# Layer 1's retention: decayed queries made by VectorE from the turned queries, scores over 128 rows of zero-padded keys, the retention's steps sooner

## The reference, cut to what matters

```
n = arange(128);  diff = n[:, None] - n[None, :]
dmat  = where(diff >= 0, exp(log_g * diff), 0)      # within a chunk
xi    = exp(log_g * (n + 1))                        # decay of a query's row
zeta  = exp(log_g * (127 - n))                      # decay of a key's row
inner = ((qc @ kc.T) * dmat) @ vc
cross = (qc * xi[:, None]) @ state
state = exp(log_g * 128) * state + (kc * zeta[:, None]).T @ vc
out   = rms(forward + backward);  mixed = out * silu(gate)
```

## Time and profile before

| what | value |
|---|---|
| median of 3 runs | 814.98 us (814.67 to 816.67) |
| span of the profiled execution | 811.6 us |
| median less span | 3.4 us |
| TensorE busy | 805.4 us, 99% |
| VectorE busy | 634.0 us, 78% |
| ScalarE busy | 339.9 us, 42% |
| GpSimd busy | 187.8 us, 23% |

### The profile page before, as it was taken

One profiled execution on the slowest core, in us unless ns is written; L12 is line 12 of the kernel. 1 busy time (PEld: TensorE's weight loads), 2 busy tenths in 40 slices (PEclk: granted clock), 3 DMA queues, 4 the chain that ended last, 5 costly groups with the idle time before them and its releaser, 6 DMA issues.

```text
span 811.6 us, 11794 instructions
## 1 busy us (share of the span) xinstructions
PE 805.4 (99%) x4364; PEld 691.4 (85%) x4364; DVE 634.0 (78%) x1112; ACT 339.9 (42%) x721; POOL 187.8 (23%) x189
## 2 busy tenths in 40 slices
PE   9999999999999999999999999999999999999998
PEld 7788888888888888888888888888889988999986
DVE  5998778768984476885578788978798678599998
ACT  4374465632122254342545544551134222455580
POOL 2222111111121221122324555544260114000000
PEclk9999999999999999999999999999999999999999
DMA  7236644445143322336868677596935634866562
GB/s 241 88 96 233 233 155 156 151 161 182 53 156 114 95 78 78 90 93 130 177 144 163 140 151 161 131 182 135 202 104 183 182 98 135 235 184 183 184 203 78
DMA packets 132862, 120.47 MB, mean 148 GB/s; under 512 B 4749, under 2 KB 100550, under 8 KB 132806
## 3 DMA queue, kind: packets, MB, share of 16 engines
q1 hardware_dynamic: 124326, 102.94, 40.9%
q0 software_dynamic: 8448, 16.78, 12.4%
q10 hardware_dynamic: 32, 0.01, 0.0%
HBM read 117.62 MB, written 35.65 MB: 189 GB/s over the span
## 4 chain that ended last, share of the span: by engine, by line
PE 92%; DVE 5%; issue 1%; ACT 1%; DMA 1%; POOL 0%; DVEq 0%; ACTq 0%
PE proj L1886 23%; PE proj L1888 23%; PE proj L1887 23%; PE bank_t L1900 3%; PE bank_o L1975 2%; DVE x L1592 1%; PE score L1888 1%; PE score L1887 1%; PE score L1886 1%; DVE w_lo L1247 1%; PE score L2050 1%; PE score L1960 1%; PE score L1961 1%; PE score L2049 1%; PE bank_o L2068 1%
## 5 line engine op out<-in xcount | busy, mean ns | idle before, releaser
L1247 DVE TENSOR_TENSOR w_lo<-w_raw,w_hi 128x1024 fp32r<-128x1024 f32 x151 | 192.0, 1274 | 44.3 <-POOL w_hi L778 36.1
L778 POOL TENSOR_SCALAR w_hi<-w_raw 128x1024 fp32r<-128x1024 f32 x101 | 118.6, 1174 | 438.6 <-DMA w_raw<-in_w_in_dram 314.6
L1886 PE MATMUL proj<-xt_hi,w_hi 128*128 128x512 f32 (+1 forms) x448 | 171.2, 382 | 0.0
L1888 PE MATMUL proj<-xt_hi,w_lo 128*128 128x512 f32 (+1 forms) x448 | 168.1, 375 | 0.0
L1887 PE MATMUL proj<-xt_lo,w_hi 128*128 128x512 f32 (+1 forms) x448 | 167.8, 374 | 0.0
L1888 PEld LDWEIGHTS proj<-xt_hi,w_lo 128*128 128x128 f32 x448 | 84.4, 188 | 15.6
L1887 PEld LDWEIGHTS proj<-xt_lo,w_hi 128*128 128x128 f32 x448 | 84.5, 189 | 14.1
L1886 PEld LDWEIGHTS proj<-xt_hi,w_hi 128*128 128x128 f32 x448 | 84.5, 189 | 14.0
L1886 PE MATMUL proj<-w_hi,xt_hi 128*128 128x512 f32 x152 | 60.9, 401 | 0.2 <-ACT prob L1012 0.2
L1888 PE MATMUL proj<-w_hi,xt_lo 128*128 128x512 f32 x152 | 59.5, 391 | 0.0
L1887 PE MATMUL proj<-w_lo,xt_hi 128*128 128x512 f32 x152 | 59.4, 391 | 0.0
(11 more groups left out here) (471 smaller groups left out, 1871.2 us busy)
## 6 DMA issues: line engine op xcount, KB each, us to landing
w_raw<-in_w_in_dram SPq DMA_DIRECT2D x79, 512.0 KB, 3.8
w_sums<-in_w_in_dram SPq DMA_DIRECT2D x8, 1024.0 KB, 7.0
w_sums<-w_sums POOLq DMA_DIRECT2D x8, 1024.0 KB, 9.1
w_raw<-w_sums SPq DMA_DIRECT2D x16, 512.0 KB, 3.8
w_raw<-w_sums SPq DMA_DIRECT2D x32, 256.0 KB, 3.3
w_raw<-in_w_out_dram SPq DMA_DIRECT2D x14, 512.0 KB, 3.3
w_raw<-in_w_in_dram SPq DMA_DIRECT2D x26, 256.0 KB, 3.3
w_sums<-in_w_attn_out_dram SPq DMA_DIRECT2D x4, 1024.0 KB, 6.5
```

What stands on the lines that cost most here:

```text
L778: pool.tensor_scalar(hi, raw, 1.0, 1.0, ALU.mult, ALU.mult).then_inc(hi_done, 1)
L1247: dve.tensor_tensor(lo, raw, hi.bitcast(F32), ALU.subtract).then_inc(w_split, 1)
L1886: pe.matmul(out, left[0], right[0], start=first, stop=False)
L1888: return pe.matmul(out, left[1], right[0], start=False, stop=last)
```

## The change

- RN 2 and 3 go, and with them `q_decay` and the four turns RT 2 to 5 of decayed queries. RT is now 0 and 1 (keys, g = 17), 2 and 3 (plain queries, g = 18).
- VectorE makes the decayed queries from the turned plain ones: for RT 2 and 3, four products each of 64 partitions by 512, PSUM bank times `decays`, a table along the tokens repeated for the four chunks. They count in `q_decayed`. In VectorE's list they stand behind AN 3.
- `decays` (2 directions, 4 heads, 128 tokens) is prepared at g = 2 and, two products for each head, at g = 4 to 10, and ScalarE takes its exponential at g = 12. `ret_c` and `steps_to` shrink accordingly; four one-column memsets for `half_of` are added at g = 2.
- ScalarE copies each bank of turned keys twice into `rk_own`, once for each of its two heads, with a scale by partition that is 1 in the head's half and 0 in the other. RS then takes all 128 rows of keys and queries.
- KV 0 waits for all four RT copies, for both `q_decayed` and for the decayed keys.
- `RET_FIRST` goes from 22 to 20, so KV, RS, RA and RB are two step times sooner; F 6 and F 7 move from g = 34 and 36 to 32 and 34, the other F stay.

```diff
-RET_FIRST = DA_STEPS + 6
+RET_FIRST = DA_STEPS + 4
...
-    if g == DA_STEPS:
-        out += [("RN", 2), ("RN", 3)]
     x = 2 * (g - DA_STEPS - 1)
-    if 0 <= x < 8:
+    if 0 <= x < 4:
         out += [("RT", x), ("RT", x + 1)]
...
-    finals = {21: 0, 22: 1, 23: 2, 25: 3, 27: 4, 29: 5, 34: 6, 36: 7}
+    finals = {21: 0, 22: 1, 23: 2, 25: 3, 27: 4, 29: 5, 32: 6, 34: 7}
...
                 act.wait_ge(rt_done, m + 1)
-                if m == 6:
+                if m == 0:
+                    act.wait_ge(halves_set, 4)
+                if m == 2:
                     act.wait_ge(av_done, DA_STEPS)
-                dst = rkT[:, m, :] if m < 2 else q_decT[:, m - 2, :] if m < 6 else rqT[:, m - 6, :]
-                act.activation(dst, score[:, m % 2, :], ACT.Copy).then_inc(rt_free, 1)
+                if m < 2:
+                    for c in range(2):
+                        last = act.activation(rk_own[:, 2 * m + c, :], score[:, m % 2, :], ACT.Copy, scale=half_of[:, c:c + 1])
+                else:
+                    last = act.activation(rqT[:, m - 2, :], score[:, m % 2, :], ACT.Copy)
+                last.then_inc(rt_free, 1)
...
+                        act.activation(decays[:], decays[:], ACT.Exp).then_inc(decay_done, 1)
...
+                for c in range(2):
+                    here, there = halves(c)
+                    dve.memset(half_of[here, c:c + 1], 1.0).then_inc(halves_set, 1)
+                    dve.memset(half_of[there, c:c + 1], 0.0).then_inc(halves_set, 1)
...
+                done(dve.tensor_scalar(decays[:, 0, last_row, :], diff[:, CENTRE:CENTRE + P], minus_p, 1.0, ALU.subtract, ALU.add))
+                done(dve.tensor_scalar(decays[:, 1, last_row, :], decays[:, 0, last_row, :], -1.0, P + 1.0, ALU.mult, ALU.add))
...
+                for c in range(2):
+                    dve.tensor_scalar(decays[:, c, h, :], decays[:, c, RET_HEADS - 1, :], log_g[:, 4 * c + h:4 * c + h + 1], None, ALU.mult)
...
+                    elif kind == "RT" and m >= 2:
+                        if m == 2:
+                            dve.wait_ge(decay_done, 3)
+                        dve.wait_ge(rt_done, m + 1)
+                        for c in range(2):
+                            here, h = slice(c * HD, (c + 1) * HD), 2 * (m - 2) + c
+                            for d in range(2):
+                                last = dve.tensor_tensor(q_decT[d * HD:(d + 1) * HD, h, :].rearrange("p (s q) -> p s q", s=ST),
+                                                         score[here, m % 2, :].rearrange("p (s q) -> p s q", s=ST),
+                                                         decays[here, d, h, :].unsqueeze(1).broadcast_to([HD, ST, P]), ALU.mult)
+                        last.then_inc(q_decayed, 1)
...
                     if m == 0:
-                        pe.wait_ge(rt_free, 8)
+                        pe.wait_ge(rt_free, 4)
+                        pe.wait_ge(q_decayed, 2)
+                        pe.wait_ge(ret_scaled, 2)
...
-                    r = slice((m % 2) * HD, (m % 2 + 1) * HD)
                     for c in range(ST):
-                        last = pe.matmul(score[:, 1, c * P:(c + 1) * P], rkT[r, m // 2, c * P:(c + 1) * P],
-                                         rqT[r, m // 2, c * P:(c + 1) * P], start=True, stop=True)
+                        last = pe.matmul(score[:, 1, c * P:(c + 1) * P], rk_own[:, m, c * P:(c + 1) * P],
+                                         rqT[:, m // 2, c * P:(c + 1) * P], start=True, stop=True)
```

More of the change, by code:

```diff
@@ L346, in build @@
         scoring.close()
-        q_decay = sb("q_decay", [P, ST, RET_HEADS, 2, HD], stack=one)
+        rk_own = sb("rk_own", [P, RET_HEADS, S], stack=one)
         q_decT = sb("q_decT", [P, RET_HEADS, S], stack=one)
@@ L369, in build @@
         diff = sb("diff", [P, TAB], stack=one)
-        rkT = sb("rkT", [P, 2, S], stack=one)
         k_decay = sb("k_decay", [P, ST, RET_HEADS, 2, HD], stack=one)
         dmat = sb("dmat", [P, RET_HEADS, P], stack=one)
+        decays = sb("decays", [P, 2, RET_HEADS, P], stack=one)
         lam_s = sb("lam_s", [P, 2], stack=one); lam_e = sb("lam_e", [P, 2], stack=one); neg_lam = sb("neg_lam", [P, 1], stack=one)
@@ L377, in build @@
         dec_z = sb("dec_z", [P, 8], stack=one); dec_q = sb("dec_q", [P, 8], stack=one); dec_p = sb("dec_p", [P, 8], stack=one)
-        log_g = sb("log_g", [P, 8], stack=one); steps_to = sb("steps_to", [P, 4], stack=one)
-        ret_c = sb("ret_c", [P, 6, RET_HEADS], stack=one); rs_k = sb("rs_k", [P, ST], stack=one)
+        log_g = sb("log_g", [P, 8], stack=one); steps_to = sb("steps_to", [P, 2], stack=one); half_of = sb("half_of", [P, 2], stack=one)
+        ret_c = sb("ret_c", [P, 4, RET_HEADS], stack=one); rs_k = sb("rs_k", [P, ST], stack=one)
         neg_log_b = sb("neg_log_b", [P, 4], stack=one)
@@ L603, in build @@
         decay_arg = sem("decay_arg"); decay_done = sem("decay_done")
-        ret_scaled = sem("ret_scaled")
+        ret_scaled = sem("ret_scaled"); q_decayed = sem("q_decayed"); halves_set = sem("halves_set")
         rt_done = sem("rt_done"); rt_free = sem("rt_free")
@@ L1306, in prepare_decays @@
                 minus_p = diff[:, CENTRE:CENTRE + 1]
-                for k, (sign, steps) in enumerate(((-1.0, 1.0), (1.0, P), (1.0, P - 1.0), (-1.0, 0.0))):
+                for c in range(2):
+                    here, there = halves(c)
+                    dve.memset(half_of[here, c:c + 1], 1.0).then_inc(halves_set, 1)
+                    dve.memset(half_of[there, c:c + 1], 0.0).then_inc(halves_set, 1)
+                for k, (sign, steps) in enumerate(((1.0, P - 1.0), (-1.0, 0.0))):
                     dve.tensor_scalar(steps_to[:, k:k + 1], minus_p, sign, float(steps), ALU.mult, ALU.add).then_inc(dve_chain, 1)
@@ L1310, in prepare_decays @@
                 dve.wait_ge(dve_chain, chain[0])
[L1311 to L1313 removed]
+                for k in range(2):
+                    dve.tensor_scalar(ret_c[:, k, :], log_g[:, 4 * k:4 * k + 4], steps_to[:, k:k + 1], None, ALU.mult)
+                last_row = RET_HEADS - 1
+                done(dve.tensor_scalar(decays[:, 0, last_row, :], diff[:, CENTRE:CENTRE + P], minus_p, 1.0, ALU.subtract, ALU.add))
+                done(dve.tensor_scalar(decays[:, 1, last_row, :], decays[:, 0, last_row, :], -1.0, P + 1.0, ALU.mult, ALU.add))
+                dve.tensor_scalar(ret_c[:, 2:4, :], log_g[:].rearrange("p (c h) -> p c h", c=2), float(P), None, ALU.mult).then_inc(decay_arg, 1)
             def prepare_matrix(h):
                 near = diff[:, CENTRE:CENTRE + P]
+                for c in range(2):
+                    dve.tensor_scalar(decays[:, c, h, :], decays[:, c, RET_HEADS - 1, :], log_g[:, 4 * c + h:4 * c + h + 1], None, ALU.mult)
                 done(dve.tensor_scalar(dmat[:, h, :], near, neg_log_b[:, h:h + 1], None, ALU.mult))
@@ L1708, in take_steps @@
                                 wait_evacuated(dve, U_RQK, j)
[L1709 to L1712, removed]
+                        dve.tensor_tensor(k_decay[:, :, :, m, :], rqk[:, :, 256:512].rearrange("p s (h d) -> p s h d", h=RET_HEADS),
+                                          ret_c[:, m, :].unsqueeze(1).unsqueeze(3).broadcast_to([P, ST, RET_HEADS, HD]),
                                           ALU.mult).then_inc(ret_scaled, 1)
+                    elif kind == "RT" and m >= 2:
[9 more added lines that the diff above has]
+                        last.then_inc(q_decayed, 1)
                     elif kind == "KV":
@@ L1727, in take_steps @@
                         for k in (1, 2):
-                            dve.scalar_tensor_tensor(out=state[k + 1][f, :], in0=state[k][f, :], scalar=ret_c[f, 4, m:m + 1],
+                            dve.scalar_tensor_tensor(out=state[k + 1][f, :], in0=state[k][f, :], scalar=ret_c[f, 2, m:m + 1],
                                                      in1=kv[k][f, :], op0=ALU.mult, op1=ALU.add)
-                            back = dve.scalar_tensor_tensor(out=state[2 - k][b, :], in0=state[3 - k][b, :], scalar=ret_c[b, 5, m:m + 1],
+                            back = dve.scalar_tensor_tensor(out=state[2 - k][b, :], in0=state[3 - k][b, :], scalar=ret_c[b, 3, m:m + 1],
                                                             in1=kv[3 - k][b, :], op0=ALU.mult, op1=ALU.add)
@@ L1991, in step @@
                             src = rqk[:, s, 256 + m * P:256 + (m + 1) * P]
-                        elif m < 6:
-                            src = q_decay[:, s, m - 2, :, :].rearrange("p c d -> p (c d)")
                         else:
-                            src = rqk[:, s, (m - 6) * P:(m - 5) * P]
+                            src = rqk[:, s, (m - 2) * P:(m - 1) * P]
                         last = pe.transpose(score[:, m % 2, s * P:(s + 1) * P], src, ident[:])
```

2 lines of the change are left out of this document (removed).

## The result

The changed kernel takes 821.91 us (median of 5 runs, 821.45 to 822.26) against 814.98 before: 6.9 us slower, ratio 1.0077 with a 95% interval of 1.0050 to 1.0103. The forecast was 818.8 with a range of 815.0 to 821.0: the sign and the stop at KV 0 with the fall of the clock came out, the time lies outside the range, and two more waits of TensorE weren't foreseen.

The account below looks back on a forecast made before the run. TensorE, busy 805.4 of 811.6 us, was taken as the bound. Turns -1.76, RS -1.16, AV 15 +0.45 and KV 0 +5.2 gave +2.7, 817.7 us; a clock fall of 1.1 made 818.8 us, range 815.0 to 821.0.

Parts of the forecast that it names:

- the stop at KV 0: TensorE at KV 0 waits for VectorE's decayed-query products, starting at 182.7 and not 177.5: 5.2 us lost (2.8 to 6.3).
- the fall of the clock: After TensorE stands at KV 0 its clock drops to the lower level: 1.1 us lost, 2.2 if twice as long.
- What bounds the kernel: TensorE never stands still in the changed stretch: instructions removed are gained, new waits lost in full, other engines count only through waits.
- AV 15's wait: AV 15 waits for ScalarE's copy into `wT`, put back by four scaled key copies: some 0.45 us lost (0.1 to 0.7).
- Rival 4: VectorE's products run while it waits for AN 3, so KV 0 finds them done: -2.5 us, 812.5 us; chance 0.08.
- rival 3: Products on 64 partitions take 0.30 us each, KV 0 waits 2.8 us, too short for the clock: 815.3 us; chance 0.07.
- Turns and RS: TensorE's own work: two pairs of turns fewer gain 1.76 us, RS on 128 rows gains 1.16 us.
- The length of a product: VectorE's eight decayed-query products take 0.61 us each whatever the partition count, 4.88 us in all; bounds 0.30 and 0.74 each.
- KV, RS and RA moved forward need the same VectorE work in the same order: Moving these retention steps sooner was taken to leave VectorE's work and order unchanged, with F steps at 22 and 23 just in time.
- Rival 5: VectorE becomes the bound behind KV 0; TensorE waits again at F 2 or KV 1, 1 to 3 us: 819.5 to 822; chance 0.10.
- The 0.5 us "allowed" for VectorE: Allowance of 0.5 us for the F steps at 22 and 23, expected to be just in time after the steps moved forward.
- The base: The sum was made on the 811.6 us profiled span and put on the 814.98 median, with 3.4 us around it untouched.

## Why the prediction was right or wrong

By the traces the change costs 8.15 us where the forecast has 3.8. The 4.3 between them are, from the table: 1.40 at the output projection and 0.95 in layer 2, both put at nothing; 0.85 in the stop and 0.72 in the clock, both there but sized too low; 0.56 at launch, which isn't the change's; and small terms.

- **What bounds the kernel** (TensorE never waits, so a new wait counts in full): right. So was the wait's place, the order of VectorE's queue that makes it, and the time of AV 15's wait (0.47 for 0.45). Rival 4 (products in VectorE's idle stretch) and rival 3 (0.30 us each) are out by the rows at 178.46.
- **Turns and RS**: -3.10 for -2.92. KV and RS take 1.78, as taken. The little more comes from around it, near the upper bound that the section gave.
- **The length of a product** is the first mis-sized term. 0.61 was taken from a row of 128 partitions, with the argument that an operation is as long as its elements in a partition however many partitions there are. Each is as long (0.69), but these eight, on 64 partitions and alternating halves, don't overlap: 0.705 from start to start, 0.76 us more in eight. The bound (0.74) held it, and the trace before had nearer rows than the one it took. Two operations of 64x512 in its layer 2, 1.51 for two of 0.75:

```profile
363.93 1.51 DVE L1665 SCALAR_TENSOR_TENSOR yc_hi<-bank_t,q2ws,yc_hi 64x512 fp32r<-64x512 f32 x2 [0.52 <-ACT yc_hi L1168]
```

- **The stop**: 6.05 for 5.2, which is the 0.76 and 0.1 of hand-over. TensorE came to KV 0 0.66 later than forecast, and VectorE to the products 0.66 late too, so that cancels.
- **The clock**: that it falls was right, its price was not: 1.8 us and not 1.1, within the 2.2 that it gave as the other end. The estimate took only the six slow loads at launch. After the stop the lower level lasts for KV 0, RS 0 and a projection matmul.
- **"KV, RS and RA moved forward need the same VectorE work in the same order"** is the step that failed outright. `RET_NORMS` hangs on `RET_FIRST`, so the norms of the retention's heads move by two step times as well. Before, VectorE empties the bank of the last gate first and a norm follows; its timeline in the kernel before:

```profile
227.64 0.69 DVE L1373 TENSOR_TENSOR gT<-proj,rs_row 128x512 f32<-128x512 f32 x1 [1.12 <-PE proj L1888]
228.24 0.68 DVE L1328 TENSOR_REDUCE rs_v<-sq 128x4 f32<-128x512 f32 x1
```

After the change a norm of 3.9 us (228.72 to 232.65) and what follows it stand ahead of the same operation:

```profile
228.72 0.68 DVE L1343 TENSOR_REDUCE rs_v<-sq 128x4 f32<-128x512 f32 x1
...
231.03 1.00 DVE L1236 SCALAR_TENSOR_TENSOR rs_y<-rs_t,rs_y 128x4 f32<-128x4 f32 x1
...
232.65 0.69 DVE L1786 TENSOR_TENSOR o_raw<-o_raw,rs_y 128x512 f32<-128x512 f32 x1
...
235.60 0.69 DVE L1388 TENSOR_TENSOR gT<-proj,rs_row 128x512 f32<-128x512 f32 x1
```

The output projection needs that bank and waits 0.9 us. The wait is there in all seven traces with the sooner steps (0.8 to 2.1 us) and in neither of the two with late ones. Rival 5 named the right engine with a chance of 0.10, and as something instead of the forecast; it came on top. The 0.5 us "allowed" for VectorE never entered the sum.
- **Layer 2**: a wait of 1.2 us 190 us behind the change, not foreseen and not explained.
- **The base**: the sum was made on one trace, 1.4 us quicker than the median, and put on the median. So the miss is 4.3 us by this pair of traces and 3.1 by the medians (821.91 for 818.8). The medians miss by less because of the pair of traces, not because the sum was better.

Where did the gain go? TensorE's own work got 3.1 us shorter, as the change says it does. VectorE's got 3.3 us longer by the page (634.0 to 637.3), but at the one place where it has no room: it idles for 4.3 us until ScalarE's squares arrive and has from then on more than TensorE gives it time for. The last experiments show both halves: the padding without the products wins 0.9 to 1.4 us (the first of these isn't told from nothing), and the products at half their length and ahead of AN 3 bring the rest to par (ratio 1.0002).

## What to carry to other kernels

When work goes from the bound engine to another one, ask whether that engine has room in this stretch, behind its last wait, and not in the whole span: VectorE, 78% busy, had no room for 5.6 us here. Moving the consumer of late work does not help when all consumers stand in one in-order queue; shorten the work, or leave it where it was. And when a step time is shifted, list everything that hangs on the constant.

## What the runs showed of the hardware

- On VectorE the four products of 128 partitions x 512 start 0.60 us apart, the eight of 64 partitions 0.705, and the operations of layer 2 above 0.755. So half the partitions don't cost less. Both rows of 64 switch halves at every operation; that this is why they cost more is suggested by the four memsets above and not tested on operations of this size.
- The granted clock fell to 0.50 in stops of TensorE of 5.9, 5.7 and 6.9 us, and in one trace also after two of 0.5 and 1.9 us that lie 7 us apart (0.61 and 0.54 on average in the two windows shown). It stayed at 1.00 through and after one of 2.8 us, and fell after one of 2.1 us elsewhere. So the length of the last stop alone doesn't tell; what else counts is open.
- A small operation of VectorE that takes 0.17 us takes 1.00 now and then (the row at 231.03 above). There a rounding of POOL's runs from 230.97 to 232.02; that it is the cause wasn't tested.
